# Fused transformer blocks on one core: landing places and rounded places of the weight ring, 5 and 3 or 6 and 2

## What is computed

```python
# first model, layer i (0: swa_mixer, 1: mla_mixer)
shift, scale, gate = jnp.split(cond @ ada_w[i] + ada_b[i], 3, axis=-1)
h = rmsnorm(x, norm_g[i]) * (1.0 + scale) + shift
x = x + gate * o                      # o: the mixer of h and of the context
...
# second model
def sqrelu_mlp(x, w_up, w_down):
    h = jax.nn.relu(x @ w_up)         # 2048 -> 8192
    return (h * h) @ w_down           # 8192 -> 2048

for i in range(DEPTH):
    h = pool_mixer(...) if i == 0 else dilated_attention(...)
    x = layer_norm(DEEPNORM_ALPHA * x + h, ln_mix_g[i], ln_mix_b[i])
    x = layer_norm(DEEPNORM_ALPHA * x + sqrelu_mlp(x, mlp_w_up[i], mlp_w_down[i]), ...)
```

## Time and profile before

| | before |
|---|---|
| median of 3 runs, us | 3628.7 (3628.15 to 3638.37) |
| the profiled execution, us | 3635.08 |
| its span on the core, us | 3633.4 |
| mean granted PE clock | 0.982 |
| PE busy | 3488.7 us, 96% |
| DVE busy | 1875.3 us, 52% |
| ACT busy | 1445.1 us, 40% |
| POOL busy | 142.8 us, 4% |
| loads of weights | 580; all transfers together 172 GB/s over the span |

### The profile page before, as it was taken

One profiled execution on the slowest core, in us unless ns is written; L12 is line 12 of the kernel. 1 busy time (PEld: TensorE's weight loads), 2 busy tenths in 40 slices (PEclk: granted clock), 3 DMA queues, 4 the chain that ended last, 5 costly groups with the idle time before them and its releaser, 6 DMA issues.

```text
span 3633.4 us, 43454 instructions
## 1 busy us (share of the span) xinstructions
PE 3488.7 (96%) x18351; PEld 2861.3 (79%) x18351; DVE 1875.3 (52%) x2616; ACT 1445.1 (40%) x1612; POOL 142.8 (4%) x82
## 2 busy tenths in 40 slices
PE   6999999899899999999999999999999999999997
PEld 2777777667787758887888888878998788888886
DVE  2433554532566655457554555464445575445545
ACT  3223334432445443444433443343343444334432
POOL 0000000000000000004000000040000050000000
PEclk8999999999999999999999999999999999999999
DMA  9433333244332255454555555545444445555553
GB/s 376 184 139 139 139 132 124 104 175 162 133 127 94 93 230 188 174 204 155 186 219 189 193 186 187 194 165 189 178 153 146 162 178 213 189 196 186 190 193 127
DMA packets 90493, 626.06 MB, mean 172 GB/s; under 512 B 10294, under 2 KB 11319, under 8 KB 17723
## 3 DMA queue, kind: packets, MB, share of 16 engines
q1 hardware_dynamic: 84752, 602.46, 45.0%
q10 hardware_dynamic: 5548, 20.83, 1.5%
HBM read 621.15 MB, written 2.10 MB: 172 GB/s over the span
## 4 chain that ended last, share of the span: by engine, by line
PE 90%; DVE 4%; ACT 2%; DMA 2%; issue 1%; ACTq 0%; DVEq 0%
PE PS L555 16%; PE PS L484 15%; PE PS L485 14%; PE PS L490 14%; PE PS L561 8%; PE PS L511 4%; PE PS L504 4%; PE PS L505 4%; PE PS L576 2%; PE PS L586 2%; DMA raw<-in_weights 2%; DVE wlo L1609 1%; PE PS L670 1%; PE PS L683 1%; ACT whi L1109 1%
## 5 line engine op out<-in xcount | busy, mean ns | idle before, releaser
L1609 DVE TENSOR_TENSOR wlo<-raw,whi 128x2048 fp32r<-128x2048 f32 (+1 forms) x484 | 1109.3, 2295 | 1165.9 <-ACT whi L1109 1155.7
L1109 ACT ACTIVATE whi<-raw 128x2048 fp32r<-128x2048 f32 (+1 forms) x484 | 911.9, 1886 | 1093.1 <-PE PS L490 635.8
L555 PE MATMUL PS<-xm,whi 128*128 128x512 f32 x2432 | 672.2, 398 | 14.8 <-DVE xm L1625 14.3
L555 PEld LDWEIGHTS PS<-xm,whi 128*128 128x128 f32 x2432 | 419.0, 190 | 74.7 <-DVE xm L1625 9.6
L561 PEld LDWEIGHTS PS<-xm,wlo 128*128 128x128 f32 x2432 | 375.8, 190 | 52.6
L484 PE MATMUL PS<-whi,hid_hi 128*128 128x512 f32 x1024 | 398.7, 389 | 0.0
L485 PE MATMUL PS<-whi,hid_lo 128*128 128x512 f32 x1024 | 398.4, 389 | 0.0
L561 PE MATMUL PS<-xm,wlo 128*128 128x256 f32 x2432 | 388.9, 282 | 0.0
L490 PE MATMUL PS<-wlo,hid_hi 128*128 128x512 f32 x1024 | 273.7, 389 | 0.0
L490 PEld LDWEIGHTS PS<-wlo,hid_hi 128*128 128x128 f32 x1024 | 192.2, 188 | 40.0
L485 PEld LDWEIGHTS PS<-whi,hid_lo 128*128 128x128 f32 x1024 | 192.3, 188 | 39.8
(11 more groups left out here) (328 smaller groups left out, 5015.8 us busy)
## 6 DMA issues: line engine op xcount, KB each, us to landing
raw<-in_weights SPq DMA_DIRECT2D x560, 1024.0 KB, 4.8
lnB<-in_ln ACTq DMA_DIRECT2D x4, 2048.0 KB, 9.1
raw<-in_weights SPq DMA_DIRECT2D x8, 768.0 KB, 4.1
X<-in_x ACTq DMA_DIRECT2D x2, 2048.0 KB, 16.1
X<-in_x ACTq DMA_DIRECT2D x4, 1024.0 KB, 15.9
raw<-in_weights SPq DMA_DIRECT2D x8, 512.0 KB, 3.7
raw<-in_weights SPq DMA_DIRECT2D x4, 640.0 KB, 3.9
out_x<-X SPq DMA_DIRECT2D x4, 512.0 KB, 3.1
```

The costliest lines, as they stand in the source:

```text
L555: mm(PS[:, b, :], high_of(n, f), x(4 * k + c).rearrange("p s t -> p (s t)"), start=(k == 0 and c == 0), stop=False, skip_group_check=True)
L1109: return f(dst, src, ACT.Copy)
L1609: v.tensor_tensor(wlo[:, n % NR, 0:w], raw[:, n % NR, 0:w], whi[:, m % NH, 0:w], ALU.subtract).then_inc(lo_done, 1)
```

## The change

```diff
--- before
+++ after
@@ -44,7 +44,7 @@
 QBW = 384
 KEYS = (P, 2 * P)
 
-NR, NH = 5, 3
+NR, NH = 6, 2
```

## The result

The changed kernel took 3712.4 us at the median of four executions (3710.25 to 3725.27). The kernel before took 3631.4 (3628.15 to 3638.37), the median of the three executions told above and one more. The ratio is 1.0229, with a 95% interval of 1.0205 to 1.0254: 81 us slower. The profiled execution took 3710.25 us, its span is 3708.6, that is 75.2 more than before, where the sum said 58.4.

The account below looks back on a forecast made before the run. The prediction took TensorE (PE) to bound the kernel, at 90% of the chain and busy 96% of the span. Its seven terms summed to +58.4 us, giving 3687 us on the median, with a range of 3665 to 3715.

Parts of the forecast that it names:

- term A: MLP up panels: PE stalls 1.25 us at 28 panel boundaries and 0.5 at four ends of halves, 37.0 us.
- term B: First half of each MLP layer: POOL's work stretches DVE's subtractions, so stalls there are longer, 8.4 us more.
- term C: Three normalisation stages: a later copy delays the chain that makes xm, 0.65 each, 2.0 us.
- term E: Transposes at MLA's start: a copy and a subtraction now stand ahead of the first tmp, 4 us, between 0 and 8.
- term F: The start: a sixth landing place removes waits for landings, -2.8 us, between -0.5 and -4.
- term D: MLA's pairs: a split double copy, three late kTp and a copy ahead of cqT_hi, 6.8 us; upper bound 16.
- term G: PE's granted clock falls behind two of the four stalls of 2.8 and 3.7 us, +3 us, between 0 and 7.
- Nothing lost: Rival: the copy is issued ahead of the evictions, no stalls, the start's gain remains, 3626 us; chance 0.06.
- The clock at every short stall: Rival: each of 28 boundary stalls of 1.25 us also loses the clock, 1.7 us more each, 3735 us; chance 0.09.
- Shorter stalls: Rival: MLP's boundary and POOL stalls at half (3664 us) or absent (3639); chance 0.06 for 3639 to 3665.

Follow-up runs that it names:

- e1: The kernel before with copies and subtractions queued as if for two rounded places, waits still for three: 3677.2 us against 3635.1, ratio 1.0113.
- e4: The changed kernel with POOL's normalisation of X cut from 512 columns to 8 in each step: 3701.0 us in one execution.
- e6: The changed kernel with the second-next tile's copy ahead of the second eviction, only in the MLP's up panels: 3667.8 us, ratio 1.0086.
- e9: The changed kernel with DVE's subtractions of tiles 68 and 69 put behind the steps that finish ckvS: 3706.6 us, ratio 1.0197 to the kernel before.
- e3: The changed kernel without the sixth landing place (5 landing, 2 rounded places, the eighth unused): 3718.4 us, ratio 1.0235.
- e7: The changed kernel with DVE held back by an added reduction ahead of 12 late subtractions in the MLP's second halves: 3746.1 us, one execution.
- e10: The changed kernel run a second time as it is, with a second trace: 3712.0 us, ratio 1.0211 to the kernel before.
- e5: The kernel before with six landing and two rounded places for the first 30 tiles only: 3630.1 us against 3635.4, ratio 0.9986.
- e8: The kernel before with 4 landing and 4 rounded places instead of 5 and 3: 3675.8 us, ratio 1.0111.

## Why the prediction was right, and where it fell short

**Boundaries between up panels (term A, 37.0).** Right in mechanism and size: 28 steps of 1.33 (POOL's share and the clock's told below) where 1.25 was said, four of 0.61 to 0.74 at the end of a half where 0.5 was, together 39.9. What it did not see is that the two parts of the change both enter: e1 shows 0.78 for the order and the rest for the longer wait. The reading "with the numbers shifted by one" was good because it holds for both at once.

**POOL (term B, 8.4).** The mechanism is confirmed by e4. The extra over 1.33 was 1.5 and 0.9 in the first layer, where 1.55 and 2.45 were said, and, less 1.7 each for the clock, 1.4 and 1.7 in the second: 5.5 in all. The second boundary of a layer was priced too high. Tiles 217 and 377 took 0.3 more than 1.33 each, but in e4 too, so that is not POOL.

**Normalisations (term C, 2.0).** Steps of 0.90, 0.50 and 0.33 at tiles 148, 150 and 151, the like in the second (1.14, 0.51, 0.33), 0.3 in the third: 4.1.

**MLA's inputs (term E, 4).** 3.5, at tiles 56 and 59 as placed. By e1, 1.8 of it is the order.

**The start (term F, -2.8).** -6.6 in the profiled execution, -4.1 as a mean of the eight traces with six places; PE's wait for the first rounded parts went from 7.7 to 5.0 us, which is about the 2.8, and the copy at 87 us has no wait for its landing any more. The rest goes with the clock in the start, which varies: up to 170 us it cost 6.7 less than before in this trace.

**MLA's pairs and latents (term D, 6.8).** This failed in size: 13.9 with the output product's first tile. Three kTp steps of 0.95 were there as said. So was the stall behind tile 71: 3.9 with a fall of the clock, and 2.38 in e6 without one, where 2.2 was said. The failing step is "one copy of 1.1 us comes ahead of cqT_hi": I followed the moved copy into ACT's queue and not to DVE, which waited for it with an unmoved subtraction. This place cost 6.4 and not 1.1, of which 3.3 are PE's standing and the rest the fall behind it (e6, e9).

**The clock (term G, +3).** Right for the boundaries, where two of four fell (3.4). Over the kernel the sum counted only those. More fell elsewhere: the stretches behind the latents' gap lost 5.1, and the stall behind tile 71 and the places at tiles 96, 115 and 348 lost 1.7 each, with the boundaries about 15 in all (the 12 beyond the boundaries are inside the 13.9 above and the 4.65 and 4.98 below). Against that, two falls of the kernel before, at 2776 and 2810 us, worth 5.1, did not come in the changed kernel, though PE's gaps there are about as long (3.10 and 2.89 us against 3.12 and 2.72). That is a gain of 4.0 at tiles 340 and 344 which no term had; in e3 and e6 these falls came as before, so it is partly luck.

**Places not in the sum.** The prediction had gone through MLP, the norms and MLA. Missed were tile 115 in the pooling mixer (4.65), tile 348 in the output product of the dilated attention (4.98) and four evictions of the dilated attention (3.5 together). The first two in the changed kernel:

```profile
1465.22 1.91 ACT L1109 ACTIVATE whi<-raw 128x2048 fp32r<-128x2048 f32 x1 [3.53 <-PE PS L490]
...
1467.16 2.29 DVE L1609 TENSOR_TENSOR wlo<-raw,whi 128x2048 fp32r<-128x2048 f32 x1 [3.15 <-ACT whi L1109]
1469.37 1.28 DVE L1625 TENSOR_TENSOR xT_lo<-PS,xT_hi 128x512 fp32r<-128x512 f32 x2
...
1470.75 0.76 PE L484 MATMUL PS<-whi,xT_hi 128*128 128x512 f32 x1 [4.76 <-DVE xT_lo L1625]
```

```profile
2881.56 2.29 DVE L1609 TENSOR_TENSOR wlo<-raw,whi 128x2048 fp32r<-128x2048 f32 x1 [1.28 <-ACT whi L1109]
...
2884.20 7.77 PE L1040 MATMUL PS<-PTd,VA 128*128 128x128 f32 x54 [3.34 <-DVE oT L2158]
```

At tile 115 nothing moved in the order. The copy only waits for PE's tile 114 now, ends up right ahead of the transposes' eviction, and its subtraction ahead of xT_lo: the gap that was 1.69 became 4.76. In e1, with the same order and the shorter wait, this step is 0.0. At tile 348 the order moved: a subtraction stands ahead of the copy of oT, and e1 has this step in full (5.15).

**The rivals.** Nothing lost: out. The clock at every short stall: out for the up panels, no fall behind any of the 1.07 us gaps, and e7 shows none up to 1.93. Shorter stalls: out, A and B together came to 45.4, as said, with A 2.9 above and B 2.9 below its part. The skill's advice cited there, the Trainium skill's "Trainium Kernel Development and Optimization", Best Practices, to double-buffer, held as far as e6 goes: two places are enough for the up panels when the order is made for two.

**The balance.** In the profiled executions the sum was 16.8 us low. More than said: 7.1 in D, 9.6 at the two missed tiles, 3.5 in the dilated attention, 2.9 in A, 2.1 in C, 0.4 in G at the boundaries, 0.6 at tiles 217 and 377, and 1.9 in SWA, which in e9 and e10 is 0.3 and so no part of the change. Less: 3.8 in the start, 2.9 in B, 0.5 in E, and 4.0 at tiles 340 and 344 by the clock. So the sum came as near as it did because what it missed, 13 at places without a term and 7 in D, was partly made up by errors the other way, the two falls of the clock among them. The medians stand 78 (e10) and 81 us apart, 3 to 6 more than the first trace has; e10's trace has 78.5, the difference being the start.

## What to carry to other kernels

A buffer fewer in a ring costs in two ways, to be looked for along the whole program: work that moves behind other work is itself late (priced from a trace by shifting the tile numbers at one boundary), and work that stands where it stood waits longer and makes late what is queued behind it, also on a third engine that waits for the moved work with an unmoved instruction. The second kind is found by asking, at each wait of the busy engine for something other than a weight tile, which copy or subtraction stands ahead of its producer. And before a place goes from one ring to another, see whether the ring that gains is short anywhere but in the start; here the place could be lent for the start alone (e5).

## What the runs showed of the hardware

- A subtraction of 128x2048 on DVE took 2.29 us with POOL's work cut to 8 columns (e4) and up to 3.37 with POOL at work on tensors of 128x512 beside it (the changed kernel).
- PE's granted clock in the second halves of the MLP kept its level of 2.4 GHz behind gaps of 1.07 to 1.93 us and lost 1.4 to 2.0 us' worth behind each of nine gaps of 2.19 to 5.48 (e7). Elsewhere gaps of 2.2 to 3.4 us did either (3.40 in the changed kernel and in e6), and in MLA it also fell behind shorter ones (0.68 and 1.18 us close together in the changed kernel, 1.43 in e8).
- The start, up to the sixth split tile, ended between 1.5 and 6.6 us earlier than in the kernel before over eight traces with six landing places in the start (for one and the same kernel 6.6 and 1.5, the changed one and e10); a change that lives in the start needs many executions.
